# Two more tiles of a gated network through seven products instead of eight, with half a norm packed into four plain tiles

## What is computed

```python
def conv_ffn(x, w_up, conv_w, w_down):          # D_MODEL 1024, D_FF 2816
    S = x.shape[1]
    u, v = jnp.split(x @ w_up, 2, axis=-1)
    up = jnp.pad(u, ((0, 0), (FFN_CONV_WIDTH - 1, 0), (0, 0)))
    u = sum(conv_w[j] * up[:, j:j + S] for j in range(FFN_CONV_WIDTH))
    return (jax.nn.gelu(u) * v) @ w_down
...
        ffn = conv_ffn(x, w_ffn_up[i], ffn_conv[i], w_ffn_down[i])
        ple = jax.nn.sigmoid(x @ w_ple_gate[i]) * (p[i] @ w_ple_proj[i])
        x = layer_norm(ALPHA * x + ffn + ple, ln_ffn_w[i], ln_ffn_b[i])
...
    h = x                                        # second block
        u = _rmsnorm(h, norm_mix_g[l])
        z = jnp.einsum('bsd,dn->bsn', u, w_in[l])
```

## Time and profile before

| what | value |
|---|---|
| median of 3 runs | 3373.0 us (3372.93 to 3374.75) |
| span of the profiled execution | 3368.5 us |
| TensorE busy | 3289.0 us (98% of the span), 19118 matmuls |
| VectorE, ScalarE, GpSimd busy | 1785.0, 1381.8, 1298.7 us |

### The profile page before, as it was taken

The page is one execution under the profiler, slowest core; times in us unless marked ns, Lnnn a source line. Parts: engine busy times, 40 slices in busy tenths (PEclk is TensorE's granted clock), DMA queues, the critical chain, the costliest instruction groups (busy, mean ns, idle before and its releaser), DMA issues.

```text
span 3368.5 us, 48408 instructions
## 1 busy us (share of the span) xinstructions
PE 3289.0 (98%) x19118; PEld 2642.8 (78%) x19118; DVE 1785.0 (53%) x2417; ACT 1381.8 (41%) x2162; POOL 1298.7 (39%) x798
## 2 busy tenths in 40 slices
PE   7999999999999999999999999999999999999998
PEld 5877787677778878888787878888886887888886
DVE  7333325545346769777784352033364256555677
ACT  5333324344324464333443355233323363444544
POOL 2322115535322756545425654211122665444102
PEclk9999999999999999999999999999999999999999
DMA  4221213222325423333563333212333432445664
GB/s 120 79 64 58 70 58 110 71 95 70 128 89 209 140 79 106 101 94 104 192 199 94 94 119 119 67 57 85 112 122 108 132 94 66 137 142 194 225 194 141
DMA packets 404639, 381.99 MB, mean 113 GB/s; under 512 B 18464, under 2 KB 322464, under 8 KB 401600
## 3 DMA queue, kind: packets, MB, share of 16 engines
q1 hardware_dynamic: 373952, 332.77, 31.7%
q10 hardware_dynamic: 30464, 46.14, 4.0%
HBM read 291.91 MB, written 86.93 MB: 112 GB/s over the span
## 4 chain that ended last, share of the span: by engine, by line
PE 46%; DVE 3%; ACT 1%; issue 1%; POOL 0%; DMA 0%; DVEq 0%; ACTq 0%
PE psum L2046 20%; PE psum L4641 10%; PE psum L2684 7%; PE psum L1664 5%; PE psum L1711 1%; PE psum L2720 1%; PE psum L1701 0%; DVE conv L3056 0%; DVE acc L4677 0%; DVE w_lo L2579 0%; PE psum L1682 0%; PE psum L1684 0%; ACT w_hi L1978 0%; PE psum L4119 0%; DVE w_raw L4592 0%
## 5 line engine op out<-in xcount | busy, mean ns | idle before, releaser
L1997 POOL TENSOR_TENSOR w_lo<-w_raw,w_hi 128x1024 fp32r<-128x1024 f32 (+1 forms) x239 | 573.6, 2400 | 1120.6 <-ACT w_hi L1978 1100.9
L1978 ACT ACTIVATE w_hi<-w_raw 128x1024 fp32r<-128x1024 f32 (+1 forms) x243 | 251.3, 1035 | 452.3 <-PE psum L2046 429.6
L281 PE MATMUL psum<-x_hi,w_hi 128*128 128x512 f32 x832 | 361.0, 434 | 8.2 <-ACT gate L325 4.3
L2046 PE MATMUL psum<-x_hi,w_hi 128*128 128x512 f32 x912 | 342.2, 395 | 5.1 <-DVE acc L4677 2.6
L2046 PE MATMUL psum<-x_hi,w_lo 128*128 128x512 f32 x912 | 337.5, 390 | 0.0
L2046 PE MATMUL psum<-x_lo,w_hi 128*128 128x512 f32 x912 | 337.5, 390 | 0.0
L281 PE MATMUL psum<-x_hi,w_lo 128*128 128x512 f32 x832 | 328.0, 394 | 0.0
L281 PE MATMUL psum<-x_lo,w_hi 128*128 128x512 f32 x832 | 327.3, 393 | 0.0
L2046 PEld LDWEIGHTS psum<-x_hi,w_hi 128*128 128x128 f32 x912 | 171.2, 188 | 45.8 <-issue 6.4
L281 PEld LDWEIGHTS psum<-x_hi,w_hi 128*128 128x128 f32 x832 | 157.2, 189 | 56.3 <-issue 20.0
L2046 PEld LDWEIGHTS psum<-x_lo,w_hi 128*128 128x128 f32 x912 | 171.7, 188 | 37.1 <-issue 1.9
(11 more groups left out here) (812 smaller groups left out, 7775.1 us busy)
## 6 DMA issues: line engine op xcount, KB each, us to landing
w_raw<-in_w_in SPq DMA_DIRECT2D x105, 512.0 KB, 4.5
merge_raw<-gates ACTq DMA_DIRECT2D x48, 512.0 KB, 4.3
x_raw<-mlp_forms SPq DMA_DIRECT2D x76, 256.0 KB, 3.3
gates<-gate SPq DMA_DIRECT2D x32, 512.0 KB, 2.9
w_raw<-in_w_mlp_out SPq DMA_DIRECT2D x54, 256.0 KB, 3.0
mlp_forms<-mlp_staged SPq DMA_DIRECT2D x13, 1024.0 KB, 3.9
w_raw<-in_w_ffn_up SPq DMA_DIRECT2D x24, 512.0 KB, 3.9
ffn_x_raw<-ffn_forms SPq DMA_DIRECT2D x46, 256.0 KB, 3.9
```

The source lines that it names most:

```text
L281: last = pe.matmul(bank, w[:, k, :], x[:, k, half(h)], start=(k == 0 and j == 0), stop=(k == KT - 1 and j == 2))
L1978: act.activation(self.view(self.c.wh, i), self.view(self.c.wr, i), ACT.Copy).then_inc(self.sig["w_hi"], 1)
L1997: pool.tensor_tensor(self.view(self.c.wl, i), self.view(self.c.wr, i), self.view(self.c.wh, i).bitcast(F32), ALU.subtract).then_inc(self.s ...
L2046: last = pe.matmul(self.bank(t, h)[0:m, :], w[:, k, col:col + m], x(k)[:, 512 * h:512 * h + 512], start=(k == 0 and n == 0), stop=(k == nk ...
```

## The change

Two hidden tiles move from the plain part to the gated one: `PAIRS` is 18, nine pairs of tiles, and four plain tiles are left. In numbers of matmuls: two more gated tiles are 2 x 84, and seven more steps of the down-projection 7 x 12; what goes is 2 tiles x 2 halves x 48 of the plain up-projection and 16 x 2 x 3 of the plain down-projection, whose strips shrink from 128x768 to 128x512. That is 2880 before and 2844 after for the whole network.

With fewer plain tiles, the norm steps of the first half get other places: the adds of the squares go to j = 0, `var` and `sd` and `scale` to j = 1, the three parts of `affine` to j = 1, 2, 3, `rms` to behind down product 1, and the eight final tiles to m = 2 to 5. The rest of the edit keeps buffers and banks in step: the two staging buffers swap, the banks of the down-projection are computed, the ninth pair's weights get a home in `x_raw` (with a wait on SyncE for the fourth product of the last gated tile, which read that space), and the place of the weights is shifted by 2 instead of 3 from block 20 on. The steps behind the change on the second half's norm stay.

```diff
-    PAIRS = 16
+    PAIRS = 18
...
-    staged = [at_(f"ffn_staged{b}", [P, 4, T // 2], F32, offset=o) for b, o in enumerate((OFF_S + 56 * KB, OFF_T + 8 * KB))]
+    staged = [at_(f"ffn_staged{b}", [P, 4, T // 2], F32, offset=o) for b, o in enumerate((OFF_T + 8 * KB, OFF_S + 56 * KB))]
...
-        w_homes = [b[:, i, :] for b in w_rows for i in range(4)]
+        w_homes = [b[:, i, :] for b in w_rows for i in range(4)] + [x_raw[:, 0, half(0)]]
...
-                    ((4, 6, 5, 3), (0, 2, 1, 7)), 0, (3, 4))
+                    [[gated.RING[(gated.product_number(LAST + 1, 0) + 4 * b + m) % 8] for m in range(4)] for b in range(2)], 0, (3, 4))
...
-        feed.skipped[down.blocks[20]] = 3
+        feed.skipped[down.blocks[20]] = 2
...
             for s in range(6, 10):
+                if s == COUNT - 1:
+                    gated.done(sp, gated.pairs[LAST][3][1])
                 down.fetch_w(sp, s)
...
                     ffn.tensor_up(pe, ffn.up(c, j), gated.left if c == 0 and j < 2 else None)
...
-                    if (c, j) == (1, 2):
+                    if (c, j) == (1, 1):
                         ln2.tensor_var(pe, 0)
                 for m in range(KT):
                     ffn.tensor_down(pe, c, m)
-                    if (c, m) == (1, 2):
+                    if (c, m) == (1, 1):
                         ln2.tensor_rms(pe, 0)
...
                     if (c, j) == (1, 0):
-                        ln2.square(act, 0, early)
+                        ln2.square(act, 0, range(KT))
                     if (c, j) == (1, 1):
-                        ln2.square(act, 0, later)
-                    if (c, j) == (1, 2):
                         ln2.sd(act, 0)
-                    if c and j >= 3:
-                        ln2.affine(act, 0, parts[j - 3])
+                    if c and j >= 1:
+                        ln2.affine(act, 0, parts[j - 1])
...
-                    if (c, m) == (1, 2):
+                    if (c, m) == (1, 1):
                         ln2.rms_sd(act, 0)
-                    if c and 3 <= m <= 6:
-                        ln2.rms_hi(act, 0, pair(m - 3))
+                    if c and 2 <= m <= 5:
+                        ln2.rms_hi(act, 0, pair(m - 2))
...
                     if (c, j) == (1, 0):
                         ln2.centre(dve, 0)
+                        ln2.add(dve, 0, "var", "sq")
                     if (c, j) == (1, 1):
-                        ln2.add(dve, 0, "var", "sq")
-                    if (c, j) == (1, 2):
                         ln2.scale(dve, 0)
```

More of the change, by code:

```diff
@@ L3492, in middle_group @@
     ident = mem("ident", [P, P])
-    ones, taps, carry = mem("ones", [P, P]), mem("taps", [P, 3, FF // P]), mem("carry", [P, 6, 2])
+    ones, taps, carry = mem("ones", [P, P]), mem("taps", [P, 3, FF // P]), mem("carry", [P, Ffn.COUNT, 2])
     w1, b1, w2, b2, g2 = (mem(n, [P, KT]) for n in ("mix_w", "mix_b", "ffn_w", "ffn_b", "rms_g"))
@@ L3563, in middle_group @@
         STEPS = range(len(down.blocks))
-        feed.skipped[down.blocks[20]] = 3
+        feed.skipped[down.blocks[20]] = 2
         st.feed = feed
         for c in range(2):
-            for j in range(6):
+            for j in range(ffn.COUNT):
                 ffn.plan_up(c, j)
@@ L3915, in _ @@
                         ln2.add(dve, 0, "rms", "sq_rms")
-                    if (c, m) == (1, 2):
+                    if (c, m) == (1, 1):
                         ln2.rms_rstd(dve, 0)
-                    if c and 3 <= m <= 6:
-                        ln2.rms_scale(dve, 0, pair(m - 3))
+                    if c and 2 <= m <= 5:
+                        ln2.rms_scale(dve, 0, pair(m - 2))
             ln2.centre(dve, 1)
```

7 lines of the change are left out of this document (3 added, 4 removed).

## The result

The changed kernel takes 3384.07 us (median of 12 runs, 3381.23 to 3389.37), the kernel before 3376.15 us in the same rounds (12 runs). The ratio is 1.0026, 95% interval 1.0018 to 1.0035. In a second set of rounds, with new traces, it is 1.0029 (1.0017 to 1.0040). By the means of the runs the change makes the kernel slower by 8.7 us in the first set and 10.4 us in the second, each within 2 us, where I had forecast +5.3 us. The measured time is also higher than the 3378 us on record because my base was low. The three runs that stood in the profile of before have a median of 3373.0 us; the kernel before has medians of 3374.1 to 3376.2 us in its sets of 12 to 29 runs.

A forecast was written before the change was run, and what follows sets the result against it. TensorE, busy almost all the span, was taken as the bound. Added waits of 13.5 us less 8.2 us saved gave +5.3 us, 3373.8 us on the profiled execution, so 3378 us; 8-in-10 range 3371.5 to 3382.5 us.

The forecast's parts named there:

- What the change saves: Whole network: 36 fewer matmuls at 0.2265 us save 8.2 us, taken in full because TensorE does not wait in the stages that grow.
- So I leave them alone: Waits of 2.5 and 2.3 us early in the seven-product stage and 2.6 us at the last adds: structures kept, no change.
- The saving is not made: Rival, 2 in 100: a longer wait at the seven-product stage's edges from the ninth pair's way out and back; 3 us lost, 3381 us.
- Item 1: First down product, first half: the last hidden tile's low part comes late, partly beside VectorE's four subtractions; wait of 1.9 us.
- item 3: Matmul of var: centring and adds take about as long as TensorE's 10.9 us of products; wait of 0.1 us.
- item 4: Third plain u strip, second half: its split stands behind sd and three affine and square pairs on ScalarE; wait of 4.5 us.
- item 7: Matmul of rms: the seven adds end 6.3 us after down product 0, with little TensorE work between; wait of 2.9 us.
- Item 2: From short strips to long, first half to second: u strip's split 0.9 us late and its DMA 0.5; sum 1.4 us.
- item 8: Final tiles: strip 4's split behind `rms_sd` 0.5 us, product 7 0.3 us, rest at the long query strip; sum 2.7 us.
- Item 6: First down product, second half: ScalarE late; 1.5 us if TensorE was slowed before, 2.6 us if not; taken as 2.0 us.
- Item 5: After the stall at the third plain u strip: halved clock, 1.7 us at most, or a late v strip, 0.5; taken as 1.0 us.
- the rival of the clock: Rival, 30 in 100: clock falls behind the rms wait too, deciding near 2.5 us; +7.5 to +10 us, 3380.5 to 3383 us.

The follow-up runs named there:

- Packed16: The kernel before, with sixteen pair tiles and six plain ones, given only the changed kernel's packed norm steps of the first half; 3380.01 us, ratio 1.0016.
- affine_later: The changed kernel with the first half's three affine parts each one step later on ScalarE; 3379.81 us, ratio 1.0015 to the kernel before.
- both_back_again: Second run of the changed kernel with affine parts one step later and the rms statistic behind the third down product; 3379.59 us, ratio 1.0014 to the kernel before.

## Why the prediction missed

The direction was right, and so were most of the waits. Two steps failed: leaving the waits of the seven-product stage alone (1.9 us), and charging only one stall with a slow clock, 1.0 us in the second half where 3.1 us were added. Of the 6.1 us between 3378 and 3384.07 us, 3.2 us are neither: they are the base, 3373.0 us in the forecast and 3376.15 us in the runs beside the changed kernel. By its own steps:

*What the change saves.* 38.2 us for two gated tiles against 38.1: taken in full, as forecast.

*"So I leave them alone."* This is the step that failed in the seven-product stage: 20.9 us instead of 19.0. I had looked only whether the structure stays, not at the store and fetch behind which the seventh step's form stands, nor at how long that wait is in other executions. It is 2.5 us before and 2.7 to 4.5 us after, with a slow clock behind the five waits from 3.6 us on and not behind the two of 2.7 and 2.8. Of the 1.9 us, 1.3 are more waiting and 0.6 more slow clock. Why the store ahead of the form lands later than before stays open. "The saving is not made" named the stage and 3 us, but gave it 2 in 100 and looked at the ninth pair's own way, not at the forms queued behind it.

*Items 1, 3, 4 and 7*, forecast 1.9, 0.1, 4.5 and 2.9 us, are 2.3, under 0.1, 4.5 and 3.0. Packed16 and affine_later show that item 4 has the cause named: the order on ScalarE. Item 1 priced the collision with VectorE at one subtraction, and it was two (0.4 us each).

*Item 2 and the first part of item 8*, the strips from short to long: 1.4 forecast, and 1.0 to 2.6 us measured at the second half's first u strip, 1.9 on the mean of twelve traces. That strip's DMA took 3.9 us in the row I used and takes 4.1 to 4.8 there, 4.4 on the mean, which is the 0.5 us that the item lacks. The row was the median of five transfers, some of them at other places. At the first query strip it is 1.9 to 2.6 us against some 1.9.

*Item 6*: 1.4 us against 2.0 (0.9 and 0.5).

*Item 5 and the rival of the clock.* I charged 1.0 us for the clock behind the wait of item 4 and nothing behind item 7. In the six traces of the changed second half the clock fell behind item 4 each time and behind the matmul of rms in four; in the other two it fell once for longer behind item 4, and once behind the first u strip. Together 2.7 to 6.5 us are lost in matmuls at the slow clock, 3.7 on the mean, where two traces with the second half of the kernel before have none and the third 1.7. Windows of TensorE in the changed kernel:

```profile
1975.30:1978.10 2.80, 2.80 (x8) 0.50 0.31 94
1998.70:2001.90 3.20, 3.20 (x9) 0.50 0.05 16
```

8 and 9 matmuls at 1.2 GHz, whose starts are some 0.43 us apart instead of 0.2265; each stretch costs about 1.6 us. That is the rival to which I gave 30 in 100, and its +7.5 to +10 us hold the 8.7 us of the first set, with 10.4 just outside; but part of the sum was the seven-product stage, which it did not name. Its threshold "near 2.5 us" was wrong as a rule: the window at 1661 us above has a slow clock behind the same 2.5 us that cost nothing in the other trace.

The stage table has 10.0 us where I had 5.3. Of the 4.7 us that the forecast lacks, 1.9 are in the seven-product stage and some 1.2 in the plain first half (0.4 of item 1, 0.5 of the late u strip, the rest short down strips). Some 1.0 are in the second half: the clock took 2.1 us more than I charged, and the waits were 1.1 us less than my items. The rest, 0.6 us, is rounding and what I took off for the slower first matmul behind a wait.

One thing stays open. The stretch ahead of the pairs is the same code, and yet it ends at 1329.4 to 1332.9 us in the four traces with sixteen pairs and at 1332.3 to 1335.6 in the twelve with eighteen, 2.6 us later on the mean. It can be chance: the four traced executions were 1.9 us faster than the mean of their kernels' runs, and the twelve 0.5 us slower. With these 2.6 us the stages would sum to +12.6 us, more than the runs give. No run tells the two apart.

## What to carry to other kernels

A change that trades cover for fewer matmuls must be reckoned on both sides: here 36 matmuls saved 8.2 us, and the packing that the shorter loop forced on the norm cost 5.1 us by itself, most of it one weight split queued behind six activations that nobody waited for yet. Put the splits that TensorE waits for ahead of the work that is due later, and give each new wait of 2 us or more a chance of a halved clock behind it (about 1.6 us here); from 3.6 us on it came every time. When a wait shrinks, look at the distance between two fixed matmuls as well: a slow clock ahead of it can shorten a wait without winning anything. A wait behind a DMA is no constant: read it in several traces before calling it unchanged.

## What was unexpected of the hardware

The clock behind a wait is not set by the wait's length alone. Over the sixteen traces, from the pairs to the first query product, I counted the waits during which, or within 2 us behind which, a stretch at 1.2 GHz began: all 14 of 3.6 us or more, 5 of the 7 near 3.0 us, 29 of the 41 of 2.4 to 2.8 us and 3 of the 12 of 2.1 to 2.3 us. It came behind a few shorter ones too, as behind 1.7 us in affine_later. Behind the last adds (2.7 to 2.8 us in every trace) 1.3 to 1.7 us were lost in eleven traces and nothing in five. TensorE's windows some 2 us behind this wait in the changed kernel and in both_back_again:

```profile
1866.00:1869.00 3.00, 3.00 (x8) 0.53 1.16 306
```

```profile
1863.00:1866.00 3.00, 3.00 (x15) 1.00 1.15 308
```

The waits at the first down product and at the third u strip, which come from the order of instructions, repeat to 0.05 us from trace to trace (2.31 us in ten traces, 4.49 to 4.53 us in eight), while those for the seventh form and for the first u strip, which end with a transfer, spread over 1.7 us. The 768 KB store took 6.4 to 8.1 us in seven traces with the same instructions issued around it, and 6.1 us in each of three traces of the other order.
